# Half of the MLP input's features by seven block products of eight, with the weight sums built in DRAM during the mixer

## The reference, cut to what matters

```
h = rms_norm(x, pre_norm_mix);   y = hybrid_mixer(h, w_in, ...)        # attention + gated DeltaNet
x = x + rms_norm(y, post_norm_mix)
h = rms_norm(x, pre_norm_mlp)
y = square(relu(h @ w_mlp_in)) @ w_mlp_out                             # 512x1024 @ 1024x4096 @ 4096x1024
x = x + rms_norm(y, post_norm_mlp)
```

## Time and profile before

| what | value |
|---|---|
| median of 3 runs | 750.02 us (748.83 to 750.32) |
| the profiled execution, its own time | 749.34 us |
| its span, first to last instruction | 747.6 us |
| TensorE busy | 740.2 us, 4168 matmuls |
| VectorE, ScalarE, GpSimd busy | 435.5, 389.5, 324.9 us |
| mean granted TensorE clock | 0.998 |
| DMA queue of SyncE (q1), of GpSimd (q0) | 109.47 MB, 18.88 MB |

### The profile page before, as it was taken

How to read it: one execution, slowest core, us unless ns; L and a number is a source line. 1 busy time by engine, 2 the same in 40 slices (tenths; PEclk the granted TensorE clock), 3 DMA queues, 4 the chain that set the end, 5 groups by cost and what they waited for, 6 DMA issues and landing times.

```text
span 747.6 us, 11913 instructions
## 1 busy us (share of the span) xinstructions
PE 740.2 (99%) x4168; PEld 607.8 (81%) x4168; DVE 435.5 (58%) x651; ACT 389.5 (52%) x632; POOL 324.9 (43%) x296
## 2 busy tenths in 40 slices
PE   9999999999999999999999999999999999999996
PEld 7788778888877878788888988888888888888885
DVE  5897899980454545444983512221221777778795
ACT  6657842268554365635655733333332655555671
POOL 2348894435454754574536466546545000000002
PEclk9999999999999999999999999999999999999999
DMA  9436224456476597276650279979978575554652
GB/s 330 113 87 211 57 71 114 127 128 150 132 171 156 169 198 197 64 160 202 210 185 28 85 233 274 238 227 294 237 227 216 159 228 194 198 184 154 220 174 114
DMA packets 86302, 129.22 MB, mean 173 GB/s; under 512 B 6096, under 2 KB 45168, under 8 KB 86256
## 3 DMA queue, kind: packets, MB, share of 16 engines
q1 hardware_dynamic: 76384, 109.47, 45.8%
q0 software_dynamic: 9536, 18.88, 14.8%
...
q10 hardware_dynamic: 336, 0.28, 0.1%
...
## 4 chain that ended last, share of the span: by engine, by line
PE 93%; POOL 3%; ACT 2%; DVE 1%; DMA 0%; issue 0%; SPq 0%; POOLq 0%; ACTq 0%; DVEq 0%
PE bank L767 28%; PE bank L768 27%; PE bank L769 27%; POOL rsq L2167 2%; PE bank L1014 1%; PE bank L1037 1%; PE bank L1024 1%; POOL w_lo L2173 1%; PE bank L978 1%; PE bank L788 1%; PE bank L942 1%; PE bank L794 1%; PE bank L989 1%; PE bank L797 0%; PE bank L1076 0%; DMA raw<-in_w_in 0%
## 5 line engine op out<-in xcount | busy, mean ns | idle before, releaser
L2173 POOL TENSOR_TENSOR w_lo<-raw,w_hi 128x512 fp32r<-128x512 f32 x169 | 219.4, 1308 | 232.7 <-ACT w_hi L1229 230.7
L1229 ACT ACTIVATE w_hi<-raw 128x512 fp32r<-128x512 f32 (+2 forms) x214 | 145.1, 684 | 154.6 <-PE bank L769 126.5
L767 PE MATMUL bank<-h_hi,w_hi 128*128 128x512 f32 (+1 forms) x528 | 208.6, 395 | 0.2
L768 PE MATMUL bank<-h_lo,w_hi 128*128 128x512 f32 (+1 forms) x528 | 204.2, 387 | 0.0
L769 PE MATMUL bank<-h_hi,w_lo 128*128 128x512 f32 (+1 forms) x528 | 204.1, 387 | 0.0
L767 PEld LDWEIGHTS bank<-h_hi,w_hi 128*128 128x128 f32 x528 | 99.2, 188 | 26.1 <-issue 5.1
L769 PEld LDWEIGHTS bank<-h_hi,w_lo 128*128 128x128 f32 x528 | 99.2, 188 | 20.5
L768 PEld LDWEIGHTS bank<-h_lo,w_hi 128*128 128x128 f32 x528 | 99.3, 188 | 18.6
L1638 DVE SCALAR_TENSOR_TENSOR relu_sb<-bank,rs_row 128x512 f32<-128x512 f32 x32 | 20.6, 686 | 126.5 <-PE bank L769 114.8
L2311 POOL TENSOR_SCALAR ssh<-ssy 128x1 f32<-128x1 f32 x4 | 1.0, 238 | 151.6 <-ACT junk L1609 151.6
L767 PE MATMUL bank<-w_hi,a_hi 128*128 128x512 f32 x120 | 46.8, 390 | 0.0
...
## 6 DMA issues: line engine op xcount, KB each, us to landing
raw<-in_w_in SPq DMA_DIRECT2D x87, 256.0 KB, 2.9
raw<-in_w_mlp_in SPq DMA_DIRECT2D x62, 256.0 KB, 4.9
t_sum<-in_w_mlp_out POOLq DMA_DIRECT2D x12, 1024.0 KB, 10.7
raw<-in_w_mlp_out SPq DMA_DIRECT2D x26, 256.0 KB, 3.1
raw<-t_sum SPq DMA_DIRECT2D x26, 256.0 KB, 3.2
v_sum<-in_w_mlp_out SPq DMA_DIRECT2D x4, 1024.0 KB, 6.5
t_sum<-in_w_mlp_out SPq DMA_DIRECT2D x4, 1024.0 KB, 7.2
v_sum<-in_w_mlp_out POOLq DMA_DIRECT2D x4, 1024.0 KB, 11.4
```

The lines of the kernel that those rows point to most:

```text
L767: pe.matmul(o, s_hi, m_hi, start=start, stop=False, skip_group_check=True)
L768: pe.matmul(o, s_hi, m_lo, start=False, stop=False, skip_group_check=True)
L1229: return a.activation(o, i_, ACT.Copy, scale=scale)
L2173: g.tensor_tensor(w_lo[:, slot, :], raw[:, slot, :], w_hi[:, slot, :].bitcast(F32), ALU.subtract).then_inc(lo_ready, 1)
```

## The change

The first 8 of the 16 groups stay as they are. The other half of the features (2048) is computed in 4 steps of 14 units. The 1024 channels and the 512 tokens are each cut in two, and so are the 2048 features; a step takes 256 features of either half, and makes seven products q1 to q7 of 512 channels by 256 features by 256 tokens instead of eight. Their operands are sums of blocks: of activations, made on VectorE in groups 4 to 7 (`t_full`, then high and low parts), and of weights, made in DRAM (`u_sum`). The four results c11, c12, c21, c22 are put together by VectorE out of the products' banks. The low parts of the weights are made by GpSimd for 4 of the 14 units of a step and by VectorE for 10.

The matmuls are 128x128 by 256 tokens in these steps, 12 to a unit as before. The eight new sum chunks (1 MB copy and 1 MB addition each) are built at units 26 to 61 of the mixer. The old ones are rearranged: six in the mixer, six in groups 2 to 7, and one each at the start of steps 1 and 2 (its addition at the eighth unit of the step), the last two in the following stage. One further addition is issued at the second unit of step 0. The residual `x_res` lies where new tiles go, so it is stored to DRAM in groups 2 and 3 and loaded again, by GpSimd, after the last step.

The core of the diff (renamed semaphores, sources of the later loads and declarations left out):

```diff
-U_M1 = U_OUT + 64
+U_S = U_OUT + 32
+STEPS_IN = 4
+PER_STEP = 14
+U_M1 = U_S + STEPS_IN * PER_STEP
-OUT_SUM_AT = {48: 0, 52: 1, 60: 2, 87: 3}
+OUT_SUM_AT = {48: 0, 60: 1, 69: 2, 78: 3}
-SUM_AT = {61: (0, 0), 65: (1, 0), 73: (2, 0), 74: (0, 1), 78: (1, 1), 86: (2, 1)}
+SUM_AT = {65: (0, 0), 73: (0, 1), 74: (1, 0), 82: (2, 0), 86: (2, 1), 87: (1, 1)}
+IN_SUM_AT = {26: (0, 0), 31: (0, 1), 36: (1, 0), 41: (2, 0), 45: (2, 1), 52: (1, 1), 56: (3, 0), 61: (3, 1)}
+IN_ADD_AT = {u + 2: chunk for u, chunk in IN_SUM_AT.items()}
-SUM_IN = {2: (0, 2), 3: (0, 3), 4: (3, 0), 5: (3, 1), 7: (2, 2), 8: (2, 3), 9: (1, 2), 10: (1, 3), 12: (3, 2), 13: (3, 3)}
+SUM_IN = {2: (0, 2), 3: (0, 3), 4: (3, 0), 5: (3, 1), 6: (1, 2), 7: (2, 2)}
+IN_PRODUCTS = ("q1", "q6", "q5", "q2", "q7", "q3", "q4")
+IN_BANK = {"q1": 0, "q2": 0, "q6": 2, "q7": 2, "q4": 2, "q5": 4, "q3": 4}
+LOW_POOL = (1, 3, 7, 11)
+LOW_DVE = tuple(v for v in range(PER_STEP) if v not in LOW_POOL)
@@ SyncE
+        for s in range(STEPS_IN):
+            for v in range(PER_STEP):
+                u = U_S + PER_STEP * s + v
+                sp_.wait_ge(*low_of(u - RAW))
+                sp_.dma_start(raw[:, u % RAW, :]..., in_source(s, v)).then_inc(raw_in[u % RAW], 16)
+                if v == 0 and s in (1, 2):
+                    q = 3 - s
+                    sp_.wait_ge(*added(q, 3))
+                    sp_.dma_start(*t_copy(q, 3)).then_inc(t_copied[q], 16)
@@ TensorE
-        with pe.Fori(1, 8) as i:
+        with pe.Fori(1, 4) as i:
             mlp_in(i, False)
+        def in_product(s, name):
+            # waits: q1 c11 of the step before, q6 c21, q5 c12, q2 the copy p1, q7 e1, q3 f, q4 c22
+            for half in range(2):
+                u = U_S + PER_STEP * s + 2 * IN_PRODUCTS.index(name) + half
+                pe.wait_ge(*low_of(u))
+                for kk in range(2):
+                    for e in range(2):
+                        c = slice(kk * 256 + e * P, kk * 256 + e * P + P)
+                        x_ = three(bank[IN_BANK[name] + e][:, 0:256], w_hi[:, u % SPL, c], w_lo[:, u % SPL, c],
+                                   *in_operand(name, 2 * half + kk), ...)
+                x_.then_inc(unit_done, 1)
@@ ScalarE
+        def mlp_in_step(s):
+            for v in range(PER_STEP):
+                u = U_S + PER_STEP * s + v
+                if u + LEAD < U_M1:
+                    split(None, (u + LEAD) % 4, 16 * loads(u + LEAD), u)
+                ...
+                if s == 0 and v == 0:
+                    copy(h_hi[:, 0:4, 256:512], t_full[3][:]).then_inc(dhi_ready, 1)
+                if v == 2:
+                    for e in range(2):
+                        copy(p1[:, e, :], bank[e][:, 0:256]).then_inc(p1_copied, 1)
+                if s and v in (3, 4):
+                    square_in(s - 1, v - 3)
@@ VectorE, step_in(s), for each v (all waits on unit_done left out)
+                v 0: c21(s - 1), two of 128x256      v 1: relu_in(s - 1), two of 128x768
+                v 4: e1, two of 128x256              v 6: f, two of 128x256
+                v 8: c11, two of 128x256             v 10: c22, two of 128x256
+                v 12: c12, two of 128x256
+                in_low(u + LEAD)                     # where unit u + 3 is VectorE's
+                if v_ in (7, 9):
+                    combine_in(6 + 2 * s + v_ // 2 - 3)
@@ GpSimd
+            if u in IN_ADD_AT:
+                g.wait_ge(t_copied[2 + order % 2], 16 * (order // 2 + 1))
+                g.dma_start(*u_add(q, chunk), accum_op=ALU.add).then_inc(...)
+        for s in range(STEPS_IN):
+            for v in range(PER_STEP):
+                if v in LOW_POOL:
+                    split(u % 4, nth(u))
+                if s == 0 and v == 1:
+                    add_sum(*SUM_IN[7])
+                if s in (1, 2) and v == 7:
+                    add_sum(3 - s, 3)
+        g.wait_ge(unit_done, U_M1)
+        for t in range(NT):
+            g.dma_start(x_res[:, t, :], x2_copy[t]).then_inc(late_in, 16)
+        ...
+        add_sum(3, 2)
```

365 lines of the change are left out of this document (288 added, 77 removed).

## The result

The changed kernel takes 773.04 us (median of 5 runs, 769.74 to 776.39), the kernel before 750.02 on the same chip: ratio 1.0317, 95% interval 1.0277 to 1.0357. It is slower by 3%, outside the predicted range. The profiled execution took 769.74 us, 20.4 more than the profiled one before (749.34).

A forecast was written before the change was run, and what follows sets the result against it. TensorE's stream of matmuls was taken as the bound. The terms, -6.3 + 0.2 + 0.3 + 4.2 + 0.5 + 0.2 + 1.1 + 0.3 = +0.5 us, gave 749.8 or 750.5 us; forecast 750.3, range 744.8 to 757.

The forecast's parts named there:

- rival 2: In the steps: four weight slots too few, loads averaging over 3.6 us; 755 us, up to 762; chance 0.25.
- Matmuls: Steps replacing eight groups: 86.96 us of matmuls removed, 672 of 0.120 us (80.64 us) added; -6.3 us.
- rival 3: In the steps: 256-token matmuls with waits between products take 0.125 us, not 0.120; +3.4 us, 753.7; chance 0.07.
- Feeding without disturbance: Steps without copies or additions: loads, splits and low parts keep up, VectorE 85% busy; 0.2 us, upper bound 2.8.
- First step: Start of step 0: 0.3 us for VectorE's leftover work, 0.5 for the addition at unit 1 meeting unit 6's load.
- Additions in the steps: Steps 1 and 2: each addition, issued at A, delays the 14th unit's load (v 13); 2.1 us each, 4.2 us.
- Copies: In the steps: a load behind a copy takes 5.4 us, under 5.9; 0.1 us each, bounds 0 and 1.5.
- Mixer: Mixer: eight more pairs without price, but GpSimd's issue delays a low part near 99 us; 1.1 us, bounds 0 and 3.
- Groups 4 to 7 and what lies ahead: Groups 4 to 7: activation sums on VectorE and copies on ScalarE fit; zero, 1 if VectorE lost its slack.
- Behind the steps: After the last step: VectorE's late low parts 0.3 us, bounds 0 and 2; additions and reloads none, at most 2.
- second price: Part of rival 2: after a wait over about 2.5 us, matmuls run at 1.2 GHz, not 2.4; some 2 us each.
- Rival 1: In the steps: loads get their share beside an addition, taking 5.8 us; 745.7 us, or 744.5; chance 0.27.

The follow-up runs named there:

- e1: The changed kernel with the three additions and two copies that run in steps 0 to 2 cut to 16 rows each: 758.42 us.
- e6: The changed kernel with four sum pairs moved to 385 to 440 us, others to groups 1 to 5, none in steps; last-stage reload and addition after twelve parts: 764.92 us.
- e2: The changed kernel with VectorE making the low part of unit 12 of a step behind c22, not ahead of it: 769.84 us.
- e15: The changed kernel with the two copies of the steps cut to 16 rows, the additions kept at 1 MB (into the chunk beside): 770.71 us.
- e11: The changed kernel with the copy of chunk (1, 3) issued behind the sixth load of step 2 instead of the first: 772.97 us.
- e3: The changed kernel with the mixer's eight copies and eight additions for the MLP input's weight sums cut to 16 rows each: 770.12 us.
- e13: e10 without sums in group 2, one pair back in the last stage, two quiet-stretch additions later, and the reload after 64 parts of the last stage: 751.35 us.
- e18: e13 with the reload after 44 parts, the groups' five additions issued in halves, and three of their sums one group later: 748.09 us.
- e10: e7's mixer and e9's squarings, with quiet-stretch additions some 10 us apart, the first pair at 331 to 350 us, one pair fewer in the groups: 753.70 us.
- e4: The changed kernel with the reload of x_res and the norm's weights moved from the start of the last stage to its end, behind two additions: 772.59 us.
- e8: The changed kernel with the reload of x_res and the last stage's two additions starting only when twelve of its parts are done: 774.38 us.
- e9: As e8, with ScalarE's four squarings of the last step's features behind the last stage's second round of splits: 772.56 us.
- e5: The changed kernel with the three chunks summed during the steps copied and added in four transfers of 256 KB each: 764.01 us.
- e7: As e6, with the mixer's first addition issued behind unit 25 and three later pairs two or three units later: 761.86 us.

## Why the prediction was wrong

Point by point, on the profiled execution: predicted +0.5 us, measured +20.4. Of the prediction's own signs, the stage of 97.4 us points to rival 2 ("over 90"), and the mixer's 3.9 us is past the 3 at which the forecast called itself wrong; no wait stood in step 3, as foreseen.

- **Matmuls, -6.3: right.** Their pitch is 0.120 us and an undisturbed step 20.16; rival 3 falls.
- **Feeding without disturbance, +0.2: right.** In steps 1 to 3 of e1 and in all four of e6 there is no wait.
- **First step, 0.3 + 0.5: measured 3.8** (three gaps). The term failed by its list of causes: only the addition at the step's second unit was counted, and the one issued at 497.06, 10.0 us ahead of the step, was left out. With the counted one cut down, e1 still lost 3.3.
- **Additions in the steps, 4.2: the step that failed most.** The two gaps behind them are 3.5 + 3.9 = 7.4 us over the pitch and the low clock adds 4.8, 12.2 in all. The load that decides was taken to be v 13's, issued at A + 2 to 2.5 and landing at A + 11.3; it was unit 12's, issued at A + 1.0 and landing at A + 9.2, which TensorE met through c22, wanted at about A + 8.7. Two things had been priced at zero: the place of c22 behind that low part and `combine` on VectorE (0.3 and 1.9 us by e2's trace), and the low clock. The text had the price for such a coupling, "each microsecond of lag above 1.4 is one of TensorE's", and took the lag of a step without additions for it.
- **Copies, 0.2: measured 0.8,** all of it at the start of step 1: the loads behind the copy took 6.2 and 6.3 us, not 5.4. The other copy cost nothing (e15, e11).
- **Mixer, 1.1: measured 3.9.** GpSimd's issue is 0.9 of it, near the 1.1 put down, but that is partly luck: it was put to the wait near 99 us, which did not grow; GpSimd's later work came a microsecond late and TensorE met it near 109 us. The five pairs between 90 and 160 us were priced at nothing from the groups' rows; here their late loads became 2.7 us behind qk_att, which falls to 0.3 when the bytes go (e3).
- **Groups 4 to 7 and what lies ahead: 0, measured 1.2,** of which 0.9 is one wait for VectorE's h_lo near 390 us. Its cause was not tried; it is there in e13 and e18 too, and absent in e10.
- **Behind the steps, 0.3 and at most 2: measured 5.0.** 4.3 are two waits: 1.6 from the reload, which was priced at none (gone in e4 and e8), and 2.7 for a_lo, of which 2.0 stay without the reload and 0.3 once ScalarE's squarings are moved too (e9). Both pass through ScalarE's queue, which the prediction did not follow there; it looked at VectorE's. The remaining 0.7 was not found.

Rival 2 comes nearest in its result (755 to 762) and in its second price. Its mechanism, the mean over the ring, is not what the two long gaps show, which stand behind single late loads; but with the same bytes in quarters e5 still lost 5.8 us more than e1, near the 7 that this mean gives, and no run rules it out for this part. Rival 1's load of 5.8 us beside an addition is refuted by four loads of 8.2 to 10.1. The rule behind it, that a DMA engine goes in turn between queues, stands in the Trainium skill also in the page "DMA: Bandwidth & Descriptors", section "Queues, rings and completion order", which says it of packets. That promises no equal share of the time, and these loads do not show one.

A wait was said to cost low clock from about 2.5 us on. In the changed kernel no low clock stands behind gaps of 3.1 (at 617 us) and 3.0 (at 136), and it does behind 3.7 and 4.1; in e1, e5 and e7 it stands behind 2.9 (at 601 us), 3.1 (at 610) and 2.3 (at 481). So it was about right, and not sharp.
